# A second attention in which five of eight head pairs are combined on VectorE alone, and three keep ScalarE's scaling and GpSimd's sum

## The reference, cut to what matters

```python
def block(args):
    q_blk, blk = args
    s = jnp.einsum('bhcqd,bhckd->bhcqk', q_blk.astype(f32), kf)
    q_pos = blk * Q_BLOCK + jnp.arange(Q_BLOCK)
    s = jnp.where(k_pos[None, :] <= q_pos[:, None], s, -1e30)
    prob = jax.nn.softmax(s, axis=-1)
    attn = prob[:, :, 0] - lam * prob[:, :, 1]
    return jnp.einsum('bhqk,bhkv->bhqv', attn, vf)
```

## Time and profile before

| | |
|---|---|
| Median of 3 runs | 1075.58 us (1075.14 to 1076.16) |
| Profiled execution | 1076.14 us |
| Its span | 1074.4 us |
| TensorE busy | 1032.1 us, 96% of the span |
| VectorE busy | 499.8 us, 47% |
| ScalarE busy | 559.5 us, 52% |
| GpSimd busy | 746.4 us, 69% |

### The profile page before, as it was taken

How to read it: one execution, slowest core, us unless ns; L and a number is a source line. 1 busy time by engine, 2 the same in 40 slices (tenths; PEclk the granted TensorE clock), 3 DMA queues, 4 the chain that set the end, 5 groups by cost and what they waited for, 6 DMA issues and landing times.

```text
span 1074.4 us, 20346 instructions
## 1 busy us (share of the span) xinstructions
PE 1032.1 (96%) x8566; PEld 865.9 (81%) x8566; DVE 499.8 (47%) x674; ACT 559.5 (52%) x890; POOL 746.4 (69%) x470
## 2 busy tenths in 40 slices
PE   7999999999999999999999999999999999999796
PEld 6888898999989969999998456699986787787675
DVE  3125175333456866511225948544468334223433
ACT  6548365444446956444543344221334468478835
POOL 5987458998866789998883175440317786998853
PEclk9999999999999999999999999999999999999999
DMA  9762445555545654655556335300004464653231
GB/s 359 273 239 77 138 157 176 190 185 193 183 161 186 200 174 157 195 181 192 185 188 236 117 132 180 119 4 4 4 11 150 152 226 137 202 164 135 98 131 76
DMA packets 46218, 168.36 MB, mean 157 GB/s; under 512 B 5648, under 2 KB 5904, under 8 KB 45872
## 3 DMA queue, kind: packets, MB, share of 16 engines
q1 hardware_dynamic: 43616, 158.02, 43.4%
q0 software_dynamic: 2512, 9.05, 2.5%
HBM read 166.00 MB, written 1.05 MB: 155 GB/s over the span
## 4 chain that ended last, share of the span: by engine, by line
PE 82%; ACT 7%; DVE 5%; POOL 2%; issue 2%; DMA 1%; SPq 0%; DVEq 0%; ACTq 0%
PE psum L480 25%; PE psum L517 19%; PE psum L739 16%; PE psum L2288 5%; PE psum L492 5%; POOL ring_r L829 2%; PE psum L288 1%; PE psum L2440 1%; ACT high_r L999 1%; DMA h<-x 1%; PE psum L2354 1%; PE psum L2022 1%; PE psum L2176 1%; ACT arena L1046 0%; PE psum L2307 0%
## 5 line engine op out<-in xcount | busy, mean ns | idle before, releaser
L829 POOL TENSOR_TENSOR ring_r<-ring,high_r 128x512 fp32r<-128x512 f32 (+1 forms) x374 | 646.1, 1760 | 152.6 <-ACT high_r L999 139.9
L999 ACT CAST high_r<-ring 128x1024 fp32r<-128x1024 f32 x250 | 258.0, 1050 | 192.8 <-DMA ring<-w 188.9
L517 PE MATMUL psum<-x_high,high_r 128*128 128x256 f32 x640 | 182.4, 285 | 2.8 <-DVE x_low L352 2.8
L517 PE MATMUL psum<-x_low,high_r 128*128 128x256 f32 x640 | 181.0, 283 | 0.0
L517 PE MATMUL psum<-x_high,ring_r 128*128 128x256 f32 x640 | 181.0, 283 | 0.0
L711 DVE TENSOR_TENSOR arena<-arena 128x512 f32<-128x512 f32 x32 | 51.4, 1606 | 181.8 <-ACT arena L687 181.7
L517 PEld LDWEIGHTS psum<-x_high,high_r 128*128 128x128 f32 x640 | 122.7, 192 | 4.1 <-issue 2.5
L517 PEld LDWEIGHTS psum<-x_low,high_r 128*128 128x128 f32 x640 | 122.7, 192 | 0.5
L517 PEld LDWEIGHTS psum<-x_high,ring_r 128*128 128x128 f32 x640 | 122.7, 192 | 0.0
L739 PE MATMUL psum<-high_r,zz_high 128*128 128x512 f32 x256 | 99.9, 390 | 1.3 <-DVE zz_low L718 1.3
L739 PE MATMUL psum<-ring_r,zz_high 128*128 128x512 f32 x256 | 99.7, 390 | 0.0
(11 more groups left out here) (363 smaller groups left out, 1868.2 us busy)
## 6 DMA issues: line engine op xcount, KB each, us to landing
ring<-w SPq DMA_DIRECT2D x288, 512.0 KB, 3.3
row<-rows POOLq DMA_DIRECT2D x14, 512.0 KB, 6.3
arena<-relt SPq DMA_DIRECT2D x2, 1536.0 KB, 13.6
h<-x SPq DMA_DIRECT2D x1, 1024.0 KB, 12.0
arena<-lora POOLq DMA_DIRECT2D x2, 512.0 KB, 5.6
out<-h SPq DMA_DIRECT2D x2, 512.0 KB, 2.6
arena<-xT SPq DMA_DIRECT2D x1, 768.0 KB, 7.2
con<-consts SPq DMA_DIRECT2D x1, 529.0 KB, 5.9
```

What stands on the lines that cost most here:

```text
L517: ins = nc.tensor.matmul(out, a, b, start=(k == 0 and q == 0), stop=(k == KT - 1 and q == 2))
L829: ins = nc.gpsimd.tensor_tensor(low(m)[:, part], raw(m)[:, part], read(high(m))[:, part], ALU.subtract)
L999: nc.scalar.copy(high(m), raw(m)).then_inc(high_made, 1)
```

## The change

Pairs 0, 2 and 4 are treated as before. For pairs 1, 3, 5, 6 and 7 ScalarE's five instructions and GpSimd's one go, and VectorE gets five right behind the reciprocal: r1 times minus lambda, the second buffer times r1 in two column ranges, and for the same ranges first buffer times r0 plus second buffer. Two `settle` waits stand between them. TensorE waits for `comb_ready` or the new `comb_dve`, by pair.

```diff
+        POOL_PAIRS = [0, 2, 4]
+        comb_dve = sem("comb_dve")
+
+        def combined(eng, g):
+            if g in POOL_PAIRS:
+                eng.wait_ge(comb_ready, POOL_PAIRS.index(g) + 1)
+            else:
+                eng.wait_ge(comb_dve, g - sum(n < g for n in POOL_PAIRS) + 1)
...
-            for until, work, i in ((8, rope, 0), (12, rope, 1), (18, combine, 0), (20, rope, 2), (21, combine, 1), (23, rope, 3),
-                                   (25, combine, 2), (27, combine, 3), (29, combine, 4), (31, combine, 5), (32, gate_rows, 0),
...
+            for until, work, i in ((8, rope, 0), (12, rope, 1), (18, combine, 0), (20, rope, 2), (23, rope, 3),
+                                   (25, combine, 2), (29, combine, 4), (32, gate_rows, 0),
...
-                if hh >= 2 and hh % 2 == 0:
+                if hh >= 2 and hh % 2 == 0 and hh // 2 - 1 in POOL_PAIRS:
...
                     if g >= 2:
-                        dve.wait_ge(comb_ready, g - 1)
+                        combined(dve, g - 2)
                     nc.vector.reciprocal(rd[g % 2], sums[:, 2 * g:2 * g + 2, :]).then_inc(rd_ready, 1)
+                    if g not in POOL_PAIRS:
+                        dve.wait_ge(rd_ready, g + 1)
+                        r1 = rd[g % 2][:, 1, :]
+                        settle(nc.vector.tensor_scalar(r1, r1, nlam, None, ALU.mult))
+                        b0, b1 = sd[:, (2 * g) % 4, :], sd[:, (2 * g + 1) % 4, :]
+                        halves = ((1, slice(0, 256)), (0, slice(256, 384)))
+                        for t, cut in halves:
+                            ins = nc.vector.tensor_scalar(b1[:, cut], b1[:, cut], rd[g % 2][:, 1, t:t + 1], None, ALU.mult)
+                        settle(ins)
+                        for t, cut in halves:
+                            ins = nc.vector.scalar_tensor_tensor(out=b0[:, cut], in0=b0[:, cut], scalar=rd[g % 2][:, 0, t:t + 1],
+                                                                 in1=b1[:, cut], op0=ALU.mult, op1=ALU.add)
+                        ins.then_inc(comb_dve, 1)
...
-                    pe.wait_ge(comb_ready, g + 1)
+                    combined(pe, g)
```

More of the change, by code:

```diff
@@ L938, in combine @@
             def combine(g):
-                pool.wait_ge(b_scaled, g + 1)
+                pool.wait_ge(b_scaled, POOL_PAIRS.index(g) + 1)
                 b0, b1 = sd[:, (2 * g) % 4, :], sd[:, (2 * g + 1) % 4, :]
@@ L951, in gate_rows @@
                                         ALU.mult).then_inc(gate_gain, 1)
-            for until, work, i in ((8, rope, 0), (12, rope, 1), (18, combine, 0), (20, rope, 2), (21, combine, 1), (23, rope, 3),
-                                   (25, combine, 2), (27, combine, 3), (29, combine, 4), (31, combine, 5), (32, gate_rows, 0),
-                                   (33, combine, 6), (34, combine, 7), (35, gate_rows, 1)):
+            for until, work, i in ((8, rope, 0), (12, rope, 1), (18, combine, 0), (20, rope, 2), (23, rope, 3),
+                                   (25, combine, 2), (29, combine, 4), (32, gate_rows, 0),
+                                   (35, gate_rows, 1)):
                 low_until(4 * W_KVQG + until)
```

## The result

| | before | after |
|---|---|---|
| Median | 1076.1 us (20 runs, lowest 1073.1) | 1082.6 us (1078.2 to 1086.0, 20 runs) |
| Ratio | 1 | 1.0049, 95% interval 1.0034 to 1.0064 |
| Profiled execution, span | 1076.14, 1074.4 us | 1080.75, 1079.0 us |
| Start of the last matmul to the end | 8.72 us | 9.67 us |

By the ratio the change makes the kernel slower by 5.3 us (3.7 to 6.9). The ratio leaves out two slow runs of the kernel before, of 1157.2 and 1716.6 us, and it is not the quotient of the two medians, which lie 6.5 us apart. Forecast was +1.3 us and, in absolute terms, 1076.9 within 1072.0 to 1078.9. The measured time lies above that range, on the side that had been given 27%; the direction was right, the size was not.

The account below looks back on a forecast made before the run. The prediction took ScalarE to limit the loop from 979 to 1009 us, with TensorE's chain behind. Terms 2.1 + 3.4 - 4.2 = +1.3 us gave 1076.9 us, range 1072.0 to 1078.9.

Parts of the forecast that it names:

- the side that had been given 27%: Whole kernel: slower by over 0.2%, made up of late GpSimd and the forecast's upper edge.
- the sum: At 1010.37 us: stalls of 2.1 and 3.4 us less 4.2 us of returned waits, +1.3 us.
- and so at the end: After 1010.37 us: the +1.3 us carries to the end unchanged, because the chain behind is TensorE's.
- scores of pair 7: TensorE in the loop: start moves from 993.30 to 998.8 us, 5.5 us later.
- The turns: VectorE beside subtracting GpSimd: each new instruction waits for one GpSimd instruction, five turns taking 6 to 7 us, not 1.7.
- Pair 3: TensorE before the product at hh = 9: a stall of 2.1 us, bounds 0 and 3.5.
- Pair 5: TensorE waits 1.8 us for pair 5, then 1.6 us more before pair 7's scores; second part's bounds 0 and 4.8.
- 4.2 us: TensorE from 998.8 us on: five earlier waits vanish and 4.2 us come back, at most 0.3 less.
- The wide scalings: 256-column VectorE scalings beside busy GpSimd: bounds 0.32 us and a full turn of 1.5; the turn was taken.
- Pairs 6 and 7: Late in the loop: pair 6 meets one or two turns, then VectorE is free; done by 1004.3 and 1008.1 us.
- the late-GpSimd rival: At 1002 to 1008 us GpSimd still subtracts: one or two further turns, +1.3 to 2.6 us, 1078.9; chance 20%.
- Pair 1: VectorE's idle time until 953.80 us: hidden, cost taken as 0, up to 1.5 us if all five took turns.

Follow-up runs that it names:

- hold: Changed kernel with TensorE's three stalls filled by 5, 5 and 7 idle transposes that nothing reads; 1082.54 us, ratio 1.0049.
- hold2: The filled stalls timed a second time, the same edit against the changed kernel; 1078.01 us, ratio 1.0016.
- aside: Changed kernel, but GpSimd waits at its old sum places until VectorE has combined each of the five pairs; 1073.15 us, ratio 0.9963.
- the two padded kernels: One-column VectorE fills near the start, 25 in the kernel before and 24 in the changed one; 1078.73 and 1078.52 us, one execution each.
- again: The changed kernel once more with no edit; 1081.56 us, ratio 1.0046.
- pair3_back: Changed kernel with pair 3 returned to ScalarE and GpSimd, pairs 1, 5, 6 and 7 staying on VectorE; 1077.91 us, ratio 1.0011.
- gain_later: Changed kernel with only GpSimd's first gate gain moved behind pair 5, two weight pieces later; 1079.56 us, ratio 1.0026.

## Why the prediction was wrong

**The failed step is the sum.** "2.1 + 3.4 - 4.2 = +1.3 us at 1010.37, and so at the end" carries the stalls through as plain waiting. It has no term for TensorE's granted clock. With the stalls filled, `hold` and `hold2` give +1.43 and +1.24 us there, which is the forecast's number; with the stalls empty the same sequence gave +4.10, +4.47, +3.71 and +3.00, 3.8 on average. In 6 of 6 profiled executions in which the wait before the scores of pair 7 stood open, 1.2 GHz followed within the loop, for 3.4 or 6.8 us; in the 6 in which it was filled or absent it did not. The prediction read the clock of 1.00 in the earlier trace rows as a fact of the loop, while TensorE had no wait over 1.51 us there and never two such close together.

The Trainium skill (TensorE: Matmul & The Clock Gate, "Part 1: The HAM clock gate") says that the array's clock is set by how busy TensorE has recently been. The traces agree: 1.69 us of work in 5.50, and a granted clock of 0.50 in the next 3.50.

**"And so at the end" failed in two smaller terms.** The first is +0.39 us, and it was a misreading. The prediction calls the output projection TensorE without a gap, from a row that starts at 1024.68. The same chain of the kernel before leaves TensorE at 1010.04, for ScalarE's squares (L1370), and runs through VectorE until 1016.77 (start, length, who):

```profile
1011.10 1.23 DVE small L1951
1012.36 0.86 DVE small L1953
1014.99 1.79 DVE arena L1970
1016.82 0.67 PE psum L227 x4
```

TensorE waits 0.73 us at 1016.82 for this work on the second gate, so what makes it longer is paid in full. In the changed kernel the wait is 1.13 us: the 128x8 scaling (L1953, now L1963) took 1.24 us beside GpSimd's subtractions, against 0.85 before and 0.52 in `aside`. The second is +0.95 us: the instruction packet among the output's, which goes with the count of VectorE's instructions, as the two padded kernels show. Added up for this pair of profiles, 1.43 + 2.67 + 0.39 + 0.95 = 5.44 us; with the average of 3.8 for the loop it is 5.2. The ratio gave 5.3 (3.7 to 6.9). The length of the half clock varies from execution to execution, and with it that term.

**The turns were right.** Seven of the ten instructions in pairs 3 and 5 took 1.31 to 1.40 us, the eighth, behind the gate gain, the 2.53 us that had been foretold; one came behind GpSimd's last subtraction (0.34 us) and one near the end of one (0.37). Pair 3: forecast 2.1 us of stall, 1.66 seen, since the fifth instruction found the subtractions over (0.34 us). Pair 5: forecast 1.8 and then 1.6 us; 1.58 and 2.23 seen. The second is longer because the norm's 128x8 scaling (L1963, 1.21 us instead of 0.17) needed a turn too, by the moment at which it came, which the prediction had not named; its bounds leave room for one turn more. The scores of pair 7 were forecast 5.5 us late and came 5.9 late. Behind them 4.2 us were forecast to come back, and in `hold` 4.5 did. That the difference agrees with the forecast within 0.1 us is in part luck, as one side was 0.45 us too small and the other 0.3. The wide scalings took 1.34 and 1.31 us: the value chosen between 0.32 and 1.5.

The rule of the Trainium skill, an exclusive lock (SBUF — State Buffer, "SBUF: two separate sides"), agrees with the form of each row: in the changed kernel's trace scalings and two-input sums wait, the reductions (1.21 us at 995.43) and PSUM copies (0.68 at 976.96) do not. By that page what starts first has the ports for its whole instruction; it says nothing on who comes next. The traces show both a turn each and one case of four in a row.

**Pairs 6 and 7** were free as predicted, GpSimd ending at 1001.55; the late-GpSimd rival did not occur. **Pair 1** cost nothing: one instruction of 1.38 us, hidden, and the scores behind it stand where they did in the loop.

**What returned.** Behind the scores of pair 7 the forecast gave 4.2 us back. At full clock (`hold`) it was 5.95 - 1.43 = 4.5; in the changed kernel 5.94 - 4.10 = 1.8, the rest eaten by the half clock. This is where the missing term sits.

**The rest of the range** was argued over who waits in the loop. Its upper end, 1078.9, was one to two more turns (the middle of +1.3 and +2.6 on the forecast); neither the clock nor the end of the program was among its bounds.

## What to carry to other kernels

Price a new stall on TensorE twice, once as waiting and once as the half clock that may follow; waits of 1.58 and 2.23 us within 5 us cost 1.6 to 2.7 us more here. When work moves to VectorE beside a GpSimd that runs without pause, give GpSimd a wait at that place: the same five instructions then took 1.6 to 1.7 us at pairs 3, 5 and 6, and by the ratios the kernel is 4.0 us faster (0.9 to 7.2) instead of 5.3 slower (3.7 to 6.9). Follow the chain of waits to the program's last instruction before calling the rest of it one engine's. And compare the two ends of a program before explaining a difference of under 1 us by its middle.

## What the runs showed of the hardware that I had not expected

- An instruction of VectorE that waits for GpSimd normally gets in behind one GpSimd instruction, but once (`again`, pair 3) a 128x2 scaling waited 5.19 us through four subtractions of 1.33 to 1.34 us, and once (`hold2`, pair 3) the same one, come 0.19 us before a subtraction's end, took 0.23 us. So the moment at which it comes counts as well.
- Waits of 1.58 and 2.23 us with 0.5 us of work between them were followed by 1.2 GHz for 3.4 us (`pair3_back`), and so were waits of 0.49 and 2.23 us (`gain_later`). With pair 3's stall ahead of the 1.58 and 2.23 us it was 6.8 us in three of four executions. 3.4 us at the lower level cost 1.5 to 1.6 us of time here. The lower level came in other places too, from one execution to the next: for 20.5 us in `hold`'s first layer, which no edit touches.
- 24 fills of one column at the program's start, in idle time, moved the end by 0.94 us. An 8 KB packet of instructions 2.0 us before the end goes with a landing of the output's 512 KB in 3.6 instead of 2.6 us. The Trainium skill (Runtime: NRT & Kernel Launch, "Instruction fetch mechanics") has each sequencer fetch its program in blocks by DMA, and calls that mostly hidden. Here it cost time where the packet fell among the last output's; and where the page gives blocks of 16 KiB, this packet has 8 KB.
